# Hybrid decoder step on one core: dilated prompt attention and prompt SSD as one unrolled stage of slots

## The reference, cut to what matters

```python
def dilated_attend(q, kb, vb, bias, valid):
    s = jnp.einsum('bthe,btnhe->bthn', q, kb, preferred_element_type=F32) * SCALE + bias.T.astype(F32)
    s = jnp.where(valid[:, None, :], s, NEG_INF)
    m = jnp.max(s, axis=-1, keepdims=True)
    p = jnp.exp(s - m)
    den = jnp.sum(p, axis=-1)
    o = jnp.einsum('bthn,btnhe->bthe', p, vb.astype(F32)) / den[..., None]
    return o, m[..., 0] + jnp.log(den)
...
def ssd_scan(x, dt, A, Bm, Cm, h0):
...
    a_cs = jnp.cumsum(a, axis=-1)
    scores = jnp.einsum('bclhn,bcshn->bhcls', Cc, Bc) * jnp.exp(segsum(a))
    y_diag = jnp.einsum('bhcls,bcshp->bclhp', scores, xd)
    decay_states = jnp.exp(a_cs[..., -1:] - a_cs)
    states = jnp.einsum('bclhn,bhcl,bclhp->bchpn', Bc, decay_states, xd)
...
    y_off = jnp.einsum('bclhn,bchpn,bhcl->bclhp', Cc, prev, jnp.exp(a_cs))
...
def ssd_mixer(z, xbc, dt_raw, conv_buf, h0, conv_w, conv_b, dt_bias, A_log, D_skip, norm_w):
...
    xbc_c = jax.nn.silu(causal_dwconv(xpad, conv_w, conv_b))
...
    y = y + D_skip.astype(F32)[:, None] * xs
    y = y.reshape(b, T, C_INNER) * jax.nn.silu(z.astype(F32))
    return rmsnorm(y, norm_w).astype(z.dtype), h_new, new_buf
```

## Time and profile before

| what | us |
|---|---|
| median of 3 runs (lowest, highest) | 3884.94 (3880.59, 3906.28) |
| the profiled execution | 3885.07 |
| its span from first to last instruction | 3883.4 |
| busy: PE, DVE, ACT, POOL | 3193.3, 1603.3, 830.1, 657.1 |
| dilated stage, from its start to the next one's | 223.4 |
| SSD stage, from its start to the next one's | 352.2 |

### The profile page before, as it was taken

How to read it: one execution, slowest core, us unless ns; L and a number is a source line. 1 busy time by engine, 2 the same in 40 slices (tenths; PEclk the granted TensorE clock), 3 DMA queues, 4 the chain that set the end, 5 groups by cost and what they waited for, 6 DMA issues and landing times. The chain is left out here.

```text
span 3883.4 us, 47996 instructions
## 1 busy us (share of the span) xinstructions
PE 3193.3 (82%) x16985; PEld 2716.7 (70%) x16985; DVE 1603.3 (41%) x2894; ACT 830.1 (21%) x1465; POOL 657.1 (17%) x406
## 2 busy tenths in 40 slices
PE   4799689779997758883068769999999599999997
PEld 3688579656664547773057668989989478787886
DVE  2112132257783433443433244544544534344444
ACT  2111111123332432220022221211211222121211
POOL 0000000024441112220022121211211022121120
PEclk8899899889997758996589989999999799999998
DMA  6422432277761221112343340111110321111111
GB/s 249 166 97 91 139 127 79 59 202 209 203 188 52 57 67 40 44 44 91 88 137 135 137 172 33 44 54 33 47 51 11 138 86 54 43 45 53 33 43 49
DMA packets 193028, 358.31 MB, mean 92 GB/s; under 512 B 72855, under 2 KB 113496, under 8 KB 186954
## 3 DMA queue, kind: packets, MB, share of 16 engines
q1 hardware_dynamic: 152899, 257.59, 21.5%
q10 hardware_dynamic: 36032, 67.68, 4.7%
q0 software_dynamic: 4016, 32.05, 2.5%
HBM read 290.92 MB, written 95.49 MB: 100 GB/s over the span
## 5 line engine op out<-in xcount | busy, mean ns | idle before, releaser
L2358 PE MATMUL cm_g_ps<-cm_h_hi,cm_up_hi 128*128 128x344 f32 (+1 forms) x880 | 312.0, 355 | 124.2 <-POOL cm_up_lo L2197 90.8
L2359 PE MATMUL cm_g_ps<-cm_h_lo,cm_up_hi 128*128 128x344 f32 (+1 forms) x880 | 309.8, 352 | 0.0
L2360 PE MATMUL cm_g_ps<-cm_h_hi,cm_up_lo 128*128 128x344 f32 (+1 forms) x880 | 309.5, 352 | 0.0
L2358 PE MATMUL cm_u_ps<-cm_h_hi,cm_up_hi 128*128 128x344 f32 (+1 forms) x880 | 306.9, 349 | 0.0
L2359 PE MATMUL cm_u_ps<-cm_h_lo,cm_up_hi 128*128 128x344 f32 (+1 forms) x880 | 305.6, 347 | 0.0
L2360 PE MATMUL cm_u_ps<-cm_h_hi,cm_up_lo 128*128 128x344 f32 (+1 forms) x880 | 305.6, 347 | 0.0
L2202 POOL TENSOR_TENSOR cm_dn_lo<-cm_dn_raw,cm_dn_hi 128x1024 fp32r<-128x1024 f32 x44 | 107.7, 2470 | 1002.7 <-ACT cm_dn_hi L2234 1002.7
L2358 PEld LDWEIGHTS cm_g_ps<-cm_h_hi,cm_up_hi 128*128 128x128 f32 x880 | 167.8, 191 | 147.5 <-issue 133.2
L2197 POOL TENSOR_TENSOR cm_up_lo<-cm_up_raw,cm_up_hi 128x2048 fp32r<-128x2048 f32 x44 | 204.2, 4643 | 285.4 <-ACT cm_up_hi L2219 285.4
L288 PE MATMUL pja_acc<-pja_w_hi,pja_h_hi 128*128 128x480 f32 (+1 forms) x512 | 198.4, 387 | 61.3 <-DVE pja_h_lo L225 61.3
L2225 ACT ACTIVATE cm_gate<-cm_g_ps 128x344 f32<-128x344 f32 (+1 forms) x110 | 55.1, 511 | 806.4 <-PE cm_g_ps L2360 805.5
(11 more groups left out here) (451 smaller groups left out, 7093.1 us busy)
## 6 DMA issues: line engine op xcount, KB each, us to landing
fp_kv<-in_fox_kv SPq DMA_DIRECT2D x256, 256.0 KB, 3.0
cm_up_raw<-in_w_up SPq DMA_DIRECT2D x44, 1024.0 KB, 4.9
cm_dn_raw<-in_w_down SPq DMA_DIRECT2D x44, 512.0 KB, 3.6
out_s_win<-in_cache POOLq DMA_DIRECT2D x1, 16376.0 KB, 32.1
proj_a<-pja_row ACTq DMA_DIRECT2D x17, 962.0 KB, 4.1
proj_b<-pjb_row ACTq DMA_DIRECT2D x17, 643.0 KB, 3.3
sp_raw<-proj_b SPq DMA_DIRECT2D x16, 640.0 KB, 4.0
dp_raw<-proj_a POOLq DMA_DIRECT2D x48, 192.0 KB, 3.3
```

The costliest lines, as they stand in the source:

```text
L2358: pe.matmul(out, hi, h_hi[:, k, cs], start=(k == 0), stop=False)
L2359: pe.matmul(out, hi, h_lo[:, k, cs], start=False, stop=False)
L2360: last = pe.matmul(out, lo, h_hi[:, k, cs], start=False, stop=(k == KT - 1))
```

## The change

Both functions are replaced by `local_stage`, in which the 48 blocks and the 16 chunks are worked together in SLOTS = 55 slots, written out in full (no loops on the chip). A slot does one step for each of four blocks that are one slot apart, and a third of the work on a chunk (phase s % 3); each engine has its own list of what a slot holds. Block u is turned in slot u+2, scored in u+3, its probabilities are turned in u+4 and its values multiplied in u+5.

- PSUM: a block has one bank (three banks in turn) that holds all its steps; the SSD part has five. A head's scores lie beside the other's in one bank, and the second head's scores wait on a semaphore (`scored_low`) for the first's.
- ACT copies q and k in one instruction (`copy_qk`, 256 columns), which is the last of its slot; the scale goes into the exponential. The copies that carried k and v to the next trip, and DVE's five small copies per chunk (`a_now`), are gone; DVE gains one small instruction per block.
- The input of a chunk is turned and convolved in the slots s//3 = c; its states and outputs come three slots later (`back`). The tanh is taken in two parts, four columns in phase 1 and three in phase 2.
- All loads and stores of both parts stand on SP's queue. The bias table's way through HBM is behind the slots 0 to 2, in which only the SSD part and block turns have work.

The diff, cut to the parts that are spoken of:

```diff
+    SLOTS = UNITS + LAG + 5
+    RAWS, OUTS, BANKS = 8, 6, 3
     CT = CONV_DIM // P
...
+        w_ps = ctx.enter_context(nc.psum_tensor("dp_w", [P, BANKS, 512], F32))
+        m_ps = ctx.enter_context(nc.psum_tensor("sp_m_ps", [P, 5, 512], F32))
+        conv_ps = m_ps[:, 0:2].rearrange("p a n -> p (a n)")
+        seg_ps = m_ps[:, 2:4, 0:HG * P]
+        st_ps, off_ps = m_ps[:, 3, 0:C_INNER], m_ps[:, 2, 0:C_INNER]
+        x_ps = m_ps[:, 4, 0:C_INNER]
+        y_ps = x_ps
+        b_ps = m_ps[:, 4, 0:C_GROUPS * C_STATE].rearrange("p (g n) -> p g n", n=C_STATE)
+        cb_ps = m_ps[:, 1, 0:C_GROUPS * P].rearrange("p (g n) -> p g n", n=P)
...
+            def store_blk(u):
+                g, i, k = place(u)
+                sp.wait_ge(o_ready, u + 1)
+                sp.wait_ge(top_ready, u + 1)
+                dst = views[g](ma[P:, :])[i, k]
+                sp.dma_start(dst[:, g * P:(g + 1) * P], out[:, u % OUTS, 0:P]).then_inc(blk_stored[u % OUTS], 16)
+                sp.dma_start(dst[:, A_WIDTH + 4 * g:A_WIDTH + 4 * g + 4], out[:, u % OUTS, P:P + 4]
+                             ).then_inc(blk_stored[u % OUTS], 16)
...
+            for s in range(SLOTS):
+                u = unit(s, 3)
+                if u is not None:
+                    copy_out(u)
+                c = chunk(s, 1, 0)
+                if c is not None:
+                    act.wait_ge(x_turned, c + 1)
+                    if c >= 1:
+                        act.wait_ge(skip_ready, c)
+                        act.wait_ge(xd_ready, c)
+                    act.activation(xs[:].rearrange("p h e -> p (h e)"), x_ps, ACT.Copy).then_inc(x_ready, 1)
...
+                c = chunk(s, 0, 0)
+                if c is not None:
+                    act.wait_ge(seg_done, c + 1)
+                    if c >= 2:
+                        act.wait_ge(mix_ready, c - 1)
+                    for g in range(C_GROUPS):
+                        last = act.activation(decay[:, c % 2, g * HG:(g + 1) * HG].rearrange("p h n -> p (h n)"),
+                                              seg_ps[:, g], ACT.Exp)
+                    last.then_inc(decay_ready, 1)
...
+                u = unit(s, 1)
+                if u is not None:
+                    exps(u)
+                c = chunk(s, 0, 0)
+                if c is not None:
+                    act.wait_ge(in_turned, c + 1)
+                    if c >= 2:
+                        act.wait_ge(conv_done, 2 * (c - 1))
+                        act.wait_ge(halo_ready, c)
+                    for b in range(2):
+                        lo, hi = 4 * b, min(4 * b + 4, CT)
+                        act.activation(xT[:, c % 2, lo:hi, C_CONV - 1:], m_ps[:, b, 0:(hi - lo) * P].rearrange(
+                            "p (c n) -> p c n", n=P), ACT.Copy).then_inc(in_ready, 1)
```

```diff
+                for half in range(2):
+                    c = chunk(s, 0, 1 + half)
+                    if c is not None:
+                        lo, hi = 4 * half, min(4 * half + 4, CT)
+                        act.wait_ge(conv_done, 2 * c + half + 1)
+                        if c >= 1:
+                            act.wait_ge(s_ready, 2 * c + half - 1)
+                        act.activation(tanh[:, lo:hi].rearrange("p c n -> p (c n)"), conv_ps[:, lo * P:hi * P], ACT.Tanh
+                                       ).then_inc(tanh_ready, 1)
+                c = chunk(s, 1, 2)
+                if c is not None:
+                    act.wait_ge(y_ready, c + 1)
+                    if c >= 1:
+                        act.wait_ge(squared, c)
+                    act.activation(sq_junk[:], y_out[:, c % 2, 0:C_INNER], ACT.Square,
+                                   accum_out=y_out[:, c % 2, C_INNER:MIX_C]).then_inc(squared, 1)
+                u = unit(s, 0)
+                if u is not None:
+                    copy_qk(u)
...
+                    activate(c, 0)
+                c = chunk(s, 1, 2)
+                if c is not None:
+                    v.wait_ge(off_ready, c + 1)
+                    v.wait_ge(y_done, c + 1)
+                    v.tensor_tensor(y[:, 1], y[:, 0], y_ps.rearrange("p (h e) -> p h e", e=HD), ALU.add
+                                    ).then_inc(y_taken, 1)
+                    v.wait_ge(y_taken, c + 1)
+                    v.wait_ge(skip_ready, c + 1)
+                    dve.link(v, v.tensor_tensor(y[:, 0], y[:, 1], skip[:], ALU.add))
+                    if c >= 2:
+                        v.wait_ge(stored[c % 2], 16 * (c // 2))
+                    v.wait_ge(z_ready, c + 1)
+                    v.scalar_tensor_tensor(out=y_out[:, c % 2, 0:C_INNER], in0=y[:, 0].rearrange("p h e -> p (h e)"),
+                                           scalar=0.5, in1=z2[:, c % 2], op0=ALU.mult, op1=ALU.mult
+                                           ).then_inc(y_ready, 1)
...
+            def score(u, h):
+                if h == 0:
+                    pe.wait_ge(qk_ready, u + 1)
+                else:
+                    pe.wait_ge(scored_low, u + 1)
+                hs = slice(h * HD, (h + 1) * HD)
+                at = w_ps[:, u % BANKS, 2 * P * h:2 * P * (h + 1)]
+                if before(u):
+                    pe.matmul(at[:, 0:P], qkT[hs, u % 4, 0], qkT[hs, (u - 1) % 4, 1], start=True, stop=True)
+                pe.matmul(at[:, P:2 * P], qkT[hs, u % 4, 0], qkT[hs, u % 4, 1], start=True, stop=True
+                          ).then_inc(scored if h else scored_low, 1)
...
+            for s in range(SLOTS):
+                now, back = s // 3, s // 3 - 1
+                u = unit(s, 1)
+                if u is not None:
+                    score(u, 0)
+                u = unit(s, 3)
+                if u is not None:
+                    value(u)
+                u = unit(s, 2)
+                if u is not None:
+                    turn_p(u)
+                u = unit(s, 1)
+                if u is not None:
+                    score(u, 1)
+                if s % 3 == 0:
+                    if 0 <= back < TILES:
+                        turn_x(back)
+                    if now < TILES:
+                        turn_in(now)
+                if s % 3 == 1 and 0 <= back < TILES:
+                    turn_b(back)
+                if s % 3 == 2 and 0 <= back < TILES:
+                    states(back)
+                u = unit(s, 0)
+                if u is not None:
+                    turn(u)
+                if s % 3 == 0 and now < TILES:
+                    if now == 0:
+                        pe.wait_ge(gates_exp, 3)
+                    segments(now)
+                if s % 3 == 1 and now < TILES:
+                    convolve(now, 0)
+                if s % 3 == 2:
+                    if now < TILES:
+                        convolve(now, 1)
+                    if 0 <= back < TILES:
+                        outputs(back)
```

In `program()`:

```diff
-        dilated_prompt(nc, pa, i["consts"], i["rel"], i["dist_prompt"], toep, ma, blocks_landed)
-        ssd_prompt(nc, pb, i["consts"], i["conv_cols"], i["conv_rows"], i["heads"], gates, mc, o["p_ssm"], o["p_conv"])
+        local_stage(nc, pa, pb, i["consts"], i["rel"], i["dist_prompt"], toep, i["conv_cols"], i["conv_rows"], i["heads"],
+                    gates, ma, mc, o["p_ssm"], o["p_conv"])
         dilated_decode(nc, pa, i["consts"], i["rel"], i["dist_sample"], caches, ma)
```

More of the change, by code:

```diff
@@ new lines, in _ @@
+            for s in range(SLOTS + 2):
+                if 3 <= s + 1 < UNITS:
+                    load_blk(s + 1)
+                c = chunk(s, -1, 0)
+                if c is not None and c >= 2:
+                    load_raw(c)
+                u = unit(s, 4)
+                if u is not None:
+                    store_blk(u)
+                c = chunk(s, 2, 0)
+                if c is not None:
+                    sp.wait_ge(squared, c + 1)
+                    sp.dma_start(mc[(c + 1) * P:(c + 2) * P, :], y_out[:, c % 2]).then_inc(stored[c % 2], 16)
@@ L1540, in _, with copy_out, exps @@
-            act.sem_inc(squared, 1)
-            over_chunks(act, ahead, body)
-            act.wait_ge(stored[0], 16 * 9)
-            act.wait_ge(stored[1], 16 * 9)
+            def copy_out(u):
+                act.wait_ge(pv, u + 1)
+                act.activation(out[:, u % OUTS, 0:P], w_ps[:, u % BANKS, 0:P], ACT.Copy).then_inc(o_ready, 1)
+            def exps(u):
+                act.wait_ge(max_ready, u + 1)
+                if u >= 2:
+                    act.wait_ge(p_turned, u - 1)
+                lo = 0 if before(u) else P
+                for h in range(2):
+                    last = act.activation(probs[:, u % 2, h, lo:], s_sb[:, u % 2, h, lo:], ACT.Exp, scale=SCALE,
+                                          bias=neg[:, u % 2, h:h + 1], accum_out=out[:, u % OUTS, P + 2 + h:P + 3 + h])
+                last.then_inc(exped, 1)
@@ L1565, in _ @@
+            last.then_inc(diag_ready, 1)
             v.wait_ge(gates_exp, 3)
[L1567 to L1579 removed]
@@ L1637, in _ @@
-            pe.wait_ge(gates_exp, 3)
```

(35 more changed lines are left out.)

802 lines of the change are left out of this document (342 added, 460 removed).

## The result

The changed kernel took 4057.49 us (median of 4 runs, 4051.25 to 4058.03) beside 3885.7 for the kernel before: a ratio of 1.0428, interval 1.0389 to 1.0467, so slower, by 172 us where 122 were forecast. Its profiled execution has a span of 4056.2 us. From its first transfer at 1222.71 to the next stage's first at 1974.08 the new stage took 751.4 us, where the two stages took 575.6: 176 us more, which is all of the difference.

The account below looks back on a forecast made before the run. Both stages were taken as bound by PE. Sixteen chunks at 43.7 us (699), -38 short blocks, -14 first chunk, +17 tail, +11 end, +22 start make 697 against 575.6: +122, so 4007 us, range 3850 to 4100.

Parts of the forecast that it names:

- The waits: PE idles for ACT's copy behind segments, half the convolution and outputs: 3.3, 1.05, 2.9 us; 7.8 per three slots with starts.
- The clock falls at the long waits: Waits of 3.3 and 2.9 us lower PE's clock in two of three slots; 43.7 us per chunk, against 31.8 at full clock.
- The rival in which it holds: PE's clock stays full despite the waits: 31.8 us per chunk, stage 523 us, total 3832; chance 0.16.
- The clock comes back in phase 2: PE at half through block and states (7.1 us), then about full (6.0): 13.1 us for the phase.
- slowest rival: PE's clock never comes back: stage 826 us, about 4135; chance 0.10 for 4090 to 4150, shared with a late queue.
- The second head waits: Dilated block scores run serially: 1.76 us at half clock against 0.86 paired; loss taken as 0.9 per block, 0.5 at full.
- The two rules of the Trainium skill: Different row tiles cannot share a PSUM bank at once, so pairing goes; transpose mode does not engage full clock, phase 0 9.5.
- Transfers, unrolled code, the bias's way through HBM at nothing: SP's single queue costs 0 to 5 us, unrolling -5 to +5, the bias table lies beside slots 0 to 2: all taken as nothing.
- No wait for maxima or POOL: PE waiting for DVE's maxima or for POOL was listed as a sign that the prediction is wrong.

Follow-up runs that it names:

- the copy first: Changed kernel with ACT's copy of q and k moved ahead of decay, tanh and square, and decay behind the turned input's copies: 3753.92 us, ratio 0.9659.
- twelve fillers: Changed kernel with twelve unread matmuls in the wait behind the segments and twelve in that behind the outputs, ACT's order kept: 3858.75 us, ratio 0.9921.
- the bias over all rows: Changed kernel with each convolution column's bias matmul using all 128 rows, zeros below the bias, instead of one row: 3889.26 us, ratio 1.0016.
- the copy late in phase 1: Kernel with ACT's copy ahead (also of the turned input's copies) and values before first-head scores, with the copy back behind tanh in phase 1: 3736.63 us.

## Why the prediction was right in kind and short in size

*The waits.* Forecast 3.3, 1.05 and 2.9 us; measured 3.07, 0.96 and 2.82 in the period shown, all for ACT's copy, 104 us in all. The chain read off rows 6 was right to a quarter of a microsecond, and so was the place of the waits.

*The clock falls at the long waits.* Right, and shown: taking the waits away (3754) or filling them (3859) gives back more than the 172 us that the change cost, and of the 296 us between the changed kernel and the one with the copy first 202 are shorter matmuls. The rival in which it holds gave 3832; with twelve fillers, which come closest to that case, it was 3859. One part of this step was wrong: the wait of 1.05 us in phase 1 was taken as too short to matter, by one gap of 1.66 us. In the kernel with twelve fillers the clock fell in 7 of 13 periods behind a wait of 0.96 us. In the changed kernel this hardly showed, since the clock was mostly low when that wait came.

*The clock comes back in phase 2.* This step failed: "half through block and states, 3.8 x 1.85 = 7.1, then about full, 6.0: 13.1". The stretch from the end of cb to the end of the outputs took 30.5 to 31.5 us at 0.50 in five of the first ten periods read, about 26 at 0.61 in four, and 17.5 at 0.99 in one; full clock is about 16.5. So the return behind the states came in four of the ten and stayed out in five; in one the clock was up already. I had read from rows 7 that convolution does not bring the clock back, and used that for phase 1 only; the second half of the convolution stands directly behind the states. In the changed kernel those ten periods took 48.5 us in the mean, where 43.7 were forecast. The slowest rival, half clock nearly throughout, forecast 4135 and lies 78 us above the measurement, my forecast 50 below: the truth is between the two.

*The second head waits.* Right in sign, too small: four serial scores were put at 1.76 us at half clock by the pace of 128-row matmuls. Those of 64 rows take 0.57 to 0.59 each there (1524.95 to 1526.10 is 1.15 for two), so 2.3, and 1.26 to 1.28 instead of 0.95 at full. For 27 blocks by 0.55 and 21 by half of that this is an estimate of 21 us, at half clock throughout, of the 50 that were missing. It is also part of why full-clock periods were 25.5 to 26.3 us and not 24.5.

*The two rules of the Trainium skill.* By the Trainium skill, different row tiles need different PSUM banks ("TensorEngine Tiling (Array Packing)", Gotcha 1: PSUM Pressure). No run tries them in one bank; the runs show what losing the overlap costs. By the Trainium skill, transposition does not engage the full clock ("TensorE: Matmul & The Clock Gate", Part 4: PE-mode transpose); the prediction named this beside the slowest rival. No run isolates it. Transposes do run at full speed while the clock is up, 0.11 us each, and for the convolution that stays at half clock the run with the bias over all rows shows another cause.

*Transfers, unrolled code, the bias's way through HBM at nothing.* Borne out for transfers: no wait of PE for one, and the stores on another queue make no difference that can be told. Unrolled against looped code was not tried by itself.

*No wait for maxima or POOL.* Right; the waits of PE are for the copy, the bias table's start and the taps' first use, and two single ones for DVE of 1.6 and 0.7 us.

## What to carry to other kernels

An instruction that another engine needs first in its next step must not be queued last behind work that waits for that engine's last step: one list's order cost 304 us here, and moving the copy ahead gave it back. Price a wait of PE by what follows it and by the waits around it: taking away the 3 us before ten microseconds of work gave 3 per chunk while the other wait stayed, and taking away the 3 us before a long stretch that did not bring the clock back gave about 12. Look for matmuls with few rows in long PE stretches: here they cost time of their own and kept a low clock low.

## What the runs showed of the hardware that was not expected

- A bias matmul of one row cost more than one of 128 rows: with it a convolution column took 1.50 us, with 128 rows 1.12, both at full clock; 2.73 and 2.13 at half.
- 30 us of block work and convolution, with PE busy but for 0.96 us and every fifth matmul of the convolution on one row, stayed at 0.50 in five of the ten periods read; with all rows in use the clock rose about 2.5 us into the convolution in the period shown.
- The clock fell not within a wait but behind it: after the 2.82 us wait that ended at 1447.25 the records are still at full speed, and from 1449 they are at half.

```profile
1447.00:1448.00 1.00, 0.75 (x5) 0.63 (x6) 0.00 (x0) 0.20 (x1) 0.00 (x0) 1.00 0.19 71
1448.00:1449.00 1.00, 1.00 (x9) 1.00 (x10) 0.00 (x0) 0.00 (x0) 0.00 (x0) 0.84 0.34 126
1449.00:1450.00 1.00, 1.00 (x6) 0.67 (x5) 0.00 (x0) 0.28 (x1) 0.00 (x0) 0.50 0.00 0
```

- A wait of 0.96 us was enough for the clock to fall in 7 of 13 periods of the kernel with twelve fillers, one of 1.02 us in the kernel with the copy first. Five waits of up to 0.6 us in the kernel with the copy late in phase 1 left it up.
- Two heads' scores from two halves of the rows, in two banks, took 0.43 us per two matmuls at half clock, and 1.14 one behind the other; whether they may overlap in one bank was not tried.
